# A two-part model on one core: memory's values computed between the last first-modulation steps, the shift turned by itself, high halves' products first

## What is computed

```python
# first block, layer 0 (and the same with c_ctx and ctx for 256 context tokens)
sh1, sc1, g1, sh2, sc2, g2 = ada_mod(c, ada_w[0], ada_b[0])     # silu(c) @ w + b, six pieces of 1024
xn = modulate(rms_norm(x, norm_mix_g[0]), sh1, sc1)             # h * (1 + scale) + shift
proj = xn @ mix_in_w[0]                                         # 1024 x 1280
...
# second block, memory of 256 tokens: its keys and values need no x
mem_n = rms_norm_2(mem, mem_kv_norm)
k = rms_norm_2((mem_n @ mem_wk).reshape(B, M, 4, 64), g_k)
v = (mem_n @ mem_wv).reshape(B, M, 4, 64)
```

## Time and profile before

| | |
|---|---|
| median of 3 runs | 2252.47 us (2251.66 to 2252.79) |
| the profiled execution | 2253.71 us |
| its span | 2251.8 us |
| PE busy | 2181.5 us (97%) |
| DVE, ACT busy | 1059.6 us (47%), 751.3 us (33%) |
| mean granted clock of PE | 0.985 |

### The profile page before, as it was taken

The page is one execution under the profiler, slowest core; times in us unless marked ns, Lnnn a source line. Parts: engine busy times, 40 slices in busy tenths (PEclk is TensorE's granted clock), DMA queues, the critical chain, the costliest instruction groups (busy, mean ns, idle before and its releaser), DMA issues.

```text
span 2251.8 us, 26108 instructions
## 1 busy us (share of the span) xinstructions
PE 2181.5 (97%) x11162; PEld 1784.2 (79%) x11162; DVE 1059.6 (47%) x1426; ACT 751.3 (33%) x1131; POOL 78.5 (3%) x76
## 2 busy tenths in 40 slices
PE   6989989999998999999999999999999999999999
PEld 4778778888887888888888888877776677888887
DVE  5757655555536333333533433363475456343322
ACT  4335332222233222232332222323456545222211
POOL 0000000000000000000111000000000002101000
PEclk9999999999998999999999999999999999999999
DMA  9430445655531323223233232333100021333322
GB/s 353 132 101 21 135 146 176 198 168 196 183 104 57 94 94 107 94 84 108 94 94 94 94 103 86 107 101 117 38 1 1 19 75 57 94 94 101 100 93 81
DMA packets 190899, 236.00 MB, mean 105 GB/s; under 512 B 4096, under 2 KB 175392, under 8 KB 190656
## 3 DMA queue, kind: packets, MB, share of 16 engines
q1 hardware_dynamic: 189696, 230.42, 31.9%
q0 software_dynamic: 1088, 3.92, 0.5%
HBM read 231.31 MB, written 2.10 MB: 104 GB/s over the span
## 4 chain that ended last, share of the span: by engine, by line
PE 88%; DVE 6%; ACT 3%; SPq 1%; DMA 1%; issue 1%; DVEq 0%; ACTq 0%
PE ps L408 25%; PE ps L410 25%; PE ps L409 25%; PE ps L681 3%; PE ps L611 2%; PE ps L716 1%; DVE wl L357 1%; ACT pr L640 1%; SPq L775 1%; PE ps L2048 1%; PE ps L2093 1%; PE ps L387 1%; DVE tmp L540 1%; ACT wh L345 1%; PE ps L501 1%
## 5 line engine op out<-in xcount | busy, mean ns | idle before, releaser
L408 PE MATMUL ps<-xh,wh 128*128 128x512 f32 x1768 | 697.5, 395 | 15.7 <-DVE xl L552 8.0
L409 PE MATMUL ps<-xl,wh 128*128 128x512 f32 x1768 | 691.5, 391 | 0.0
L410 PE MATMUL ps<-xh,wl 128*128 128x512 f32 x1768 | 691.4, 391 | 0.0
L357 DVE TENSOR_TENSOR wl<-raw,wh 128x2048 fp32r<-128x2048 f32 (+1 forms) x170 | 379.0, 2230 | 483.2 <-ACT wh L345 483.1
L345 ACT CAST wh<-raw 128x2048 fp32r<-128x2048 f32 (+1 forms) x170 | 314.5, 1850 | 330.2 <-PE ps L410 254.3
L408 PEld LDWEIGHTS ps<-xh,wh 128*128 128x128 f32 x1768 | 333.4, 189 | 90.6 <-issue 15.1
L410 PEld LDWEIGHTS ps<-xh,wl 128*128 128x128 f32 x1768 | 333.2, 188 | 70.9
L409 PEld LDWEIGHTS ps<-xl,wh 128*128 128x128 f32 x1768 | 333.4, 189 | 70.5 <-issue 1.4
L408 PE MATMUL ps<-hh,wh 128*128 128x512 f32 x704 | 274.2, 389 | 0.0
L410 PE MATMUL ps<-hh,wl 128*128 128x512 f32 x704 | 274.0, 389 | 0.0
L409 PE MATMUL ps<-hl,wh 128*128 128x512 f32 x704 | 274.0, 389 | 0.0
(11 more groups left out here) (341 smaller groups left out, 1804.8 us busy)
## 6 DMA issues: line engine op xcount, KB each, us to landing
raw<-in_ffn_w SPq DMA_DIRECT2D x52, 1024.0 KB, 5.4
raw<-in_ada_w SPq DMA_DIRECT2D x40, 1024.0 KB, 5.4
raw<-in_ffn_wg SPq DMA_DIRECT2D x22, 1024.0 KB, 5.4
raw<-in_ffn_wu SPq DMA_DIRECT2D x22, 1024.0 KB, 5.4
raw<-in_ffn_w SPq DMA_DIRECT2D x16, 896.0 KB, 4.9
raw<-in_ffn_wd SPq DMA_DIRECT2D x16, 896.0 KB, 4.9
raw<-in_w_in SPq DMA_DIRECT2D x10, 1024.0 KB, 5.3
raw<-in_ffn_wd SPq DMA_DIRECT2D x8, 1024.0 KB, 5.3
```

Source lines behind the costliest of these rows:

```text
L357: e.tensor_tensor(wl[s][:, 0:n], r[:, 0:n], wh[s][:, 0:n].bitcast(F32), ALU.subtract).then_inc(*WLO.up(i))
L408: e.matmul(dst, ah, bh, start=start, stop=False)
L409: e.matmul(dst, ah, bl, start=False, stop=False)
L410: return e.matmul(dst, al, bh, start=False, stop=stop)
```

## The change

Three edits. (1) In pe_proj2 the four products with the high half of a chunk of x (two blocks of columns, high and low half of the weights) come ahead of the wait for its low half, and the two with the low half behind it. (2) Memory's values: both token blocks now go into bank 2 side by side and stand between and behind pe_first(6) and pe_first(7); ACT copies them in one instruction behind the weights of the second input unit, and PE's third block of columns waits for that copy. (3) ACT copies the shift's rows as soon as pe_first(3) is done, PE turns them behind pe_first(4), DVE adds the bias ahead of the first input unit's low half; for the scale the same follows pe_first(7), with value products around it. Both copies are ACT's now, into `acc`.

```diff
 def pe_proj2(e, banks, u, src_h, src_l, stage, keys):
             hi, lo = halves(u)
             for k in range(NC):
+                e.wait_ge(*AX[stage, k])
+                for cc in range(2):
+                    for w in (hi, lo):
+                        e.matmul(pb[banks[cc]], w[:, k, cc * P:(cc + 1) * P], src_h[:, k, :], start=k == 0 and w is hi, stop=False)
                 split_ready(e, stage, k)
                 for cc in range(2):
-                    m = mm3(e, pb[banks[cc]], hi[:, k, cc * P:(cc + 1) * P], lo[:, k, cc * P:(cc + 1) * P],
-                            src_h[:, k, :], src_l[:, k, :], k == 0, k == NC - 1)
+                    m = e.matmul(pb[banks[cc]], hi[:, k, cc * P:(cc + 1) * P], src_l[:, k, :], start=False, stop=k == NC - 1)
...
 def act_prologue(e):
             act_root(e, "x", 3, 1, T, D)
-            for tb in range(2):
-                e.wait_ge(*MM["vm", tb])
-                e.copy(vm[:, tb, :], pb[2 - 2 * tb][:, 0:256]).then_inc(*AE.up(("vm", tb)))
+            e.wait_ge(*MM["first", 3])
+            e.copy(acc[:, 0:512], pb[4]).then_inc(*AE.up(("first rows", 0)))
             act_root(e, ("km", 0), 1, 2, LC, 64)
             act_root(e, ("km", 1), 2, 2, LC, 64)
             act_weights(e, of["in", 0])
             e.wait_ge(*MM["first", 7])
-            e.copy(tmp[3][:, :], pb[3]).then_inc(*AE.up("first rows"))
+            e.copy(acc[:, 512:1024], pb[3]).then_inc(*AE.up(("first rows", 1)))
             act_norm(e, "x", xh, T, lambda c: ada[0][:, c:c + 1])
             act_weights(e, of["in", 1])
-            act_squares(e, "ctx", ctT, LC, LAND["ctx"]["ctx"], VX["x", 7], MM["first turned"])
+            e.wait_ge(*MM["vm"])
+            e.copy(vm[:, :, :], pb[2].rearrange("p (t d) -> p t d", t=2)).then_inc(*AE.up("vm"))
+            act_squares(e, "ctx", ctT, LC, LAND["ctx"]["ctx"], VX["x", 7], None)
...
 def dve_prologue(e):
+            dve_first(e, 0)
             dve_units(e, of["in", 0])
-            e.wait_ge(*MM["first", 7])
-            e.tensor_copy(ssum[:, :], pb[4]).then_inc(*VF.up("first rows"))
-            e.wait_ge(*MM["first turned"])
...
-            e.wait_ge(*VF["first", 0])
+            dve_first(e, 1)
+            e.wait_ge(*VF["first", 1, 0])
             dve_factors(e, 0, "gm0", ada[0], 1, "x")
...
 def pe_prologue(e):
             pe_proj(e, 1, 0, P, mh, ml, n=LC).then_inc(*MM.up(("km", 1), ("w", 0)))
-            e.wait_ge(*WLO[1])
-            pe_proj_tok(e, 2, 1, 0, 256, mh, ml, 0).then_inc(*MM.up(("vm", 0)))
             for n in (2, 3):
                 pe_first(e, n)
             e.wait_ge(*VF["square", "x", 7])
             pe_sums(e, "x", ssum, 1, T)
-            e.wait_ge(*AF["square", "km", 0])
-            pe_proj_tok(e, 0, 1, 0, 256, mh, ml, 1).then_inc(*MM.up(("vm", 1), ("w", 1)))
             e.wait_ge(*VF["inverse", "x"])
             pe_spread(e, "x", 3, 1, T, 5)
+            e.wait_ge(*AF["square", "km", 0])
             pe_sums(e, ("km", 0), tmp[0], 2, LC)
             pe_first(e, 4)
+            pe_first_turned(e, 0)
...
             pe_first(e, 6)
+            e.wait_ge(*WLO[1])
+            pe_proj_tok(e, 2, 1, 0, 256, mh, ml, 0, range(4))
             pe_first(e, 7)
-            pick = cst[:, CST["pick"]:CST["pick"] + 4]
-            for j, (src, ready) in enumerate(((ssum, VF["first rows"]), (tmp[3], AE["first rows"]))):
-                e.wait_ge(*ready)
...
-            m.then_inc(*MM.up("first turned"))
+            pe_proj_tok(e, 2, 1, 0, 256, mh, ml, 0, range(4, 6))
+            pe_first_turned(e, 1)
+            pe_proj_tok(e, 2, 1, 0, 256, mh, ml, 0, range(6, 8))
+            pe_proj_tok(e, 2, 1, 0, 256, mh, ml, 1, o=256).then_inc(*MM.up("vm", ("w", 1)))
...
 def pe_mix_in(e):
+                    if c == 2:
+                        e.wait_ge(*AE["vm"])
```

More of the change, by code:

```diff
@@ L429, in pe_proj2, with pe_proj_tok @@
             for k in range(NC):
+                e.wait_ge(*AX[stage, k])
+                for cc in range(2):
+                    for w in (hi, lo):
+                        e.matmul(pb[banks[cc]], w[:, k, cc * P:(cc + 1) * P], src_h[:, k, :], start=k == 0 and w is hi, stop=False)
                 split_ready(e, stage, k)
                 for cc in range(2):
-                    m = mm3(e, pb[banks[cc]], hi[:, k, cc * P:(cc + 1) * P], lo[:, k, cc * P:(cc + 1) * P],
-                            src_h[:, k, :], src_l[:, k, :], k == 0, k == NC - 1)
+                    m = e.matmul(pb[banks[cc]], hi[:, k, cc * P:(cc + 1) * P], src_l[:, k, :], start=False, stop=k == NC - 1)
                     if k == NC - 1:
                         m.then_inc(*MM.up(keys[cc], *([("w", u)] if cc else [])))
-        def pe_proj_tok(e, bank, u, c0, cols, src_h, src_l, tb):
+        def pe_proj_tok(e, bank, u, c0, cols, src_h, src_l, tb, ks=range(NC), o=0):
             hi, lo = halves(u)
             s = slice(tb * P, (tb + 1) * P)
-            for k in range(NC):
-                m = mm3(e, pb[bank][:, 0:cols], src_h[:, k, s], src_l[:, k, s], hi[:, k, c0:c0 + cols], lo[:, k, c0:c0 + cols],
+            for k in ks:
+                m = mm3(e, pb[bank][:, o:o + cols], src_h[:, k, s], src_l[:, k, s], hi[:, k, c0:c0 + cols], lo[:, k, c0:c0 + cols],
                         k == 0, k == NC - 1)
@@ L827, in act_prologue, with dve_first @@
             e.wait_ge(*MM["first", 7])
-            e.copy(tmp[3][:, :], pb[3]).then_inc(*AE.up("first rows"))
+            e.copy(acc[:, 512:1024], pb[3]).then_inc(*AE.up(("first rows", 1)))
             act_norm(e, "x", xh, T, lambda c: ada[0][:, c:c + 1])
             act_weights(e, of["in", 1])
-            act_squares(e, "ctx", ctT, LC, LAND["ctx"]["ctx"], VX["x", 7], MM["first turned"])
+            e.wait_ge(*MM["vm"])
+            e.copy(vm[:, :, :], pb[2].rearrange("p (t d) -> p t d", t=2)).then_inc(*AE.up("vm"))
+            act_squares(e, "ctx", ctT, LC, LAND["ctx"]["ctx"], VX["x", 7], None)
+        def dve_first(e, j):
+            e.wait_ge(*MM["first turned", j])
+            for z, dst in ((0, ada[0]), (1, adac)):
+                e.tensor_tensor(dst[:, 8 * j:8 * j + 8].rearrange("p (h c) -> p h c", h=2),
+                                pb[4 - j][:, 0:16].rearrange("p (c h z) -> p z h c", c=4, h=2)[:, z],
+                                v_("ab0", 8 * j, 8).rearrange("p (h c) -> p h c", h=2), ALU.add).then_inc(
+                                    *VF.up(("first", j, z)))
         def dve_prologue(e):
@@ L845, in dve_prologue @@
                 dve_head_scaled(e, ("km", c), kmT[:, c, :], v_("gmk"), LC)
+            dve_first(e, 0)
             dve_units(e, of["in", 0])
-            e.wait_ge(*MM["first", 7])
-            e.tensor_copy(ssum[:, :], pb[4]).then_inc(*VF.up("first rows"))
-            e.wait_ge(*MM["first turned"])
[L850 to L853, removed]
-            e.wait_ge(*VF["first", 0])
+            dve_first(e, 1)
+            e.wait_ge(*VF["first", 1, 0])
             dve_factors(e, 0, "gm0", ada[0], 1, "x")
-            e.wait_ge(*VF["first", 1])
+            e.wait_ge(*VF["first", 1, 1])
             dve_factors(e, 8, "gm0", adac, 1, "ctx")
@@ L883, in pe_first, with pe_first_turned @@
             m.then_inc(*MM.up(("first", n)))
+        def pe_first_turned(e, j):
+            pick = cst[:, CST["pick"]:CST["pick"] + 4]
+            e.wait_ge(*AE["first rows", j])
+            for c in range(4):
+                o = j * 512 + c * P
+                m = e.matmul(pb[4 - j][:, c * 4:c * 4 + 4], acc[:, o:o + P], pick, start=True, stop=True)
+            m.then_inc(*MM.up(("first turned", j)))
         def pe_prologue(e):
```

3 lines of the change are left out of this document (removed).

## The result

| | changed kernel | kernel before |
|---|---|---|
| median | 2261.67 us (2258.7 to 2265.07, 6 runs) | 2252.57 us (2251.66 to 2255.0, 6 runs) |
| ratio, 95% interval | 1.0033 (1.0022 to 1.0045) | |
| profiled execution, span | 2265.07 us, 2263.1 us | 2253.71 us, 2251.8 us |
| mean granted clock | 0.981 | 0.985 |

The change makes the kernel slower by 9.1 us in this comparison, outside the range of the prediction (to 2258.0), on the side of rival B. The profiled execution is the slowest of the six, so its trace may show more of the losses than a usual execution has.

What follows compares the result with a forecast made beforehand. TensorE, busy 2181.5 of 2251.8 us, was taken as the bound. The median 2252.47 plus 1.9 us for scaling delayed by a clock lost near 33 us gave 2254.4 us, range 2249.5 to 2258.0.

Steps and rivals of the forecast that it cites:

- rival B: Prologue: the fallen clock stays half through pe_first 7, scaling starts at 55.4, +6.1 us, 2258.6 us; chance 0.12.
- the mechanism and its place: Prologue: the clock falls near 33 us after the values leave, and the short steps behind run at half clock.
- when the clock returns: Prologue: back at about 46.8 us, scaling starts +2.6 us late; back at 43.4, +1.2 us.
- the term +1.9: Prologue: delay of scaling's start in us, taken between +1.2 and +2.6 since no row tells when the clock returns.
- each case is good to 1 or 2 us: Behind the prologue: later clock falls and returns can cost or save 1 or 2 us in each case.
- the chain to the end of the mixer's input: From scaling to the context's spread and the end: the end moves by what scaling's start moves.
- the high halves pay nothing: First stage and first two feed-forward stages: high-half products first add nothing; upper bound 0.9 us in each feed-forward stage.
- A: Prologue: full clock all along, scaling starts at 47.25 instead of 49.31, -2.05 us, 2250.4 us; chance 0.22.
- C: Context's spread: PE waits 2.2 us, half clock behind it takes 1.6 us of the gain back, 2252.0 us; chance 0.10.

Runs made afterwards that it cites:

- pinned: 24 products of 256 columns added in the sparse attention's first ten steps: kernel before 2256.3 us, changed kernel 2261.6 us.
- edit 2 alone: Kernel before with only memory's values moved, both halves of the rows still turned together: 2257.67 us, ratio 1.0008.
- all 39 products: Changed kernel with 39 thrown-away products where PE idles in the prologue: 2255.11 us, ratio 1.0002; with the sparse attention's added products too, 2255.67 us.
- values back: Changed kernel with memory's values and their copies in the old places: 2253.58 us, ratio 0.9993; with the sparse attention's added products too, 2256.22 us.

## Why the prediction was wrong

*Right: the mechanism and its place.* The clock fell at about 34 (forecast near 33), behind the stretch that the values left. All four traces of kernels whose stretch was emptied lost it there; the three traces with it filled did not, nor did those with the values in their old places. The steps at half clock were priced well: the spread at 34.6 (34.2 forecast), pe_first 4 at 37.3 (36.8), the shift's turning at 39.2 (38.5), pe_first 5 at 41.8 (41.1), pe_first 6 at 46.4 (45.7).

*Wrong: when the clock returns.* This is the step that failed. "If it returns at about 46.8" and "at 43.4" were the two ends, and the term +1.9 lay between. The clock returned at about 51 in the first trace, 44 in the second, 51 in the changed kernel with the pinned attention, 48 with edit 2 alone. So the term measured about 5.3 us (pinned; scaling 5.2, 1.7, 4.6 and 3.3 us late in the four traces) instead of 1.9. The late end is rival B, which had 0.12. B forecast scaling at 55.4 and the trace has 54.5, though the clock stayed at half for 5 us behind pe_first 6's start and not for the 8 that B asked for. No row of before told when a clock returns under short steps, and the term should have run to B's +6.1: in three of the four traces the clock came back later than the later of the two ends.

*Wrong: "each case is good to 1 or 2 us".* This was the term for falls further on. In the sparse attention half clock lasted 3.4 us at a time in some traces and 17 and 31 us at a stretch in others, which moves this stage alone by up to 8.2 us; single executions of the kernel before itself span 2250.5 to 2261.7 us. The three runs at hand, within 1.1 us, had not shown it. The first comparison's 9.1 us probably holds some of that besides the prologue's 5, for its one trace had the stage at its longest. The 17 us also come without the change; whether the change makes the 31 us likelier was not settled.

*Right: the chain to the end of the mixer's input.* It moved with scaling's start (5.2 late at 54.5, 5.4 late at 88.4), and with the values moved pe_first 7 never came before 44.4. Further on the two traces did not keep that distance: it was 3.1 us at 1454.

*Right: the high halves pay nothing.* Alone they gave 0.9995, and in the feed-forward stage PE's wait moved from x (2.54 to 1.75 us) to the weights (0.55 to 1.35), the sum being the same.

*In part right, and not seen in the first trace: A and C.* With the clock held, scaling starts at 47.68 at best and at 48.5 or 48.7 with all 39 products, and C's wait at the context's spread came (2.1 to 2.6 us), with half clock behind it in some traces. But A's 2.05 us was too large: it was counted from 49.31, in a trace whose clock fell inside the turning, while the kernel before started scaling at 48.47, 49.24 and 49.31 in its three traces, pinned or not. Against these the gain lies between -0.2 and 1.6 us. The pinned kernels gained 0.1 (values back), 0.4 and 0.7 us at the end, hardly to be told from zero. So even without the clock's fall in the emptied stretch the change would have been worth little.

The page of the Trainium skill (TensorE: Matmul & The Clock Gate, "Why this matters for your kernels") puts the fall down to idle gaps between bursts. The trace agrees only in part. The fall at 34 does stand behind gaps, of 1.49, 2.00 and 0.57 us with sparse steps between, and filling the first two prevents it; but the prediction read the page as letting such short gaps pass, and by that the clock would have stayed full.

## What to carry to other kernels

Work of TensorE that nobody waits for can be what holds its clock: before moving it out of a stretch of waits and small products, look at what is left there, and count half clock for the short steps that follow. Under sums, spreads and turnings it lasted from 10 to 17 us in the four traces here, and no row of the kernel before told which. What helped was dense work put ahead of these steps, in the waits; the same kind of work behind them came too late. Where single executions of a kernel spread by some us, find the stretch whose clock differs between traces, and hold it there in both kernels before judging a change of a few us. And take the starting point of a forecast gain from more than one trace: the 2.05 us here were counted from the latest of three.

## What the runs showed of the hardware that was not expected

At half clock PE can be busy without a break, 30.60 of 30.60 us in the sparse attention, and the clock stays at half; the same code in another execution loses it for 3.4 us. What stands ahead of the fall does not tell the two apart: PE was busy for 2.09 of 3.5 us in both (1607.7 to 1611.2 in the changed kernel, 1603.0 to 1606.5 before). A busy column that looks well can therefore be a stretch at half clock, as the 16.90 of 16.90 us were, and only the granted clock beside it shows that.

Adding work made a kernel faster: 26 products of 256 columns, some 3 us of PE's time where it would idle, took the changed kernel's loss of 5.3 us away, as far as two pinned comparisons on two chips can tell.
